# Splitting the next chunk's weights between the first chunk's tiles in a fused four-layer step

## Chip, cores and metric

The kernel runs on one core of a Trainium2 chip. The metric is the device time of one execution in microseconds. The time before is the median of three runs.

## What is computed

One inference step of a four-layer hybrid diffusion backbone on 128 context tokens and 512 latent tokens, model width 1024, all in fp32 accuracy. Layer 0 mixes tokens by pooling; layers 1 to 3 by attention (grouped-query, differential, windowed with a sink); each layer ends in a gated ConvFFN. The change touches the QKV projection of the three attention layers:

```python
qkv = h @ w_qkv                      # (640, 1024) @ (1024, 1536), and 3072 columns in layer 2
q, k = rmsnorm(q, qn), rmsnorm(k, kn)   # per head of 64
q, k = apply_rope(q, cos, sin), apply_rope(k, cos, sin)   # latent tokens only
```

## The kernel before

**Products.** Each fp32 product is made of three matmuls in a reduced format: `h_hi * w_hi`, `h_hi * w_lo` and `h_lo * w_hi`, where `hi` is the rounded value and `lo` what is left over. Weights come in chunks of 512 columns. A chunk is held as `UNITS` = 8 units of 128 partitions by 512 columns, one for each of the `KT` = 8 steps `k` of the contraction. ScalarE (ACT) writes `w_hi` of a unit as a rounded copy of `w_stage` (`split_w`, L2247), and VectorE (DVE) writes `w_lo` as `w_stage - w_hi` (`lo_w`, L2398). There is one buffer each for `w_stage`, `w_hi` and `w_lo`.

**QKV on TensorE (PE).** The 640 tokens are `NT` = 5 tiles of 128: tile 0 is the context, tiles 1 to 4 are latent. Layers 1 and 3 have 3 chunks (`QKV_CHUNKS`), layer 2 has 6. Tiles are counted on over the chunks: `i = c * NT + j`, and tile `i` goes to bank `i % 4` of `psA`. The first four tiles of the first chunk are computed side by side, step by step as `h` comes from the normalisation, and so end at once. From tile 4 on (token tile `j` = 4 of chunk 0) PE takes a tile at a time, 24 matmuls of 128x512 each (L2094, L2095, L2100). Tile `i` waits for the evacuation of tile `i - 4` (`s_qe`). At `j` = 0 each step `k` also waits for the `w_lo` of its unit (`s_wlo`). After step `k` of the last tile of a chunk PE raises `s_wused`, which says that unit `k` may be overwritten by the next chunk's.

**QKV on ACT.** For each tile in order: wait until it is computed, square it into `qkv_sq` (L2315, two buffers; the square of the normed tile `i` waits for the means of `i - 2`), and copy it from PSUM (L2316), which raises `s_qe`. Ahead of the last tile of a chunk come all eight `split_w` of the next chunk, each with a wait for its `s_wused`.

**QKV on DVE (`qkv_dve`, L1465).** For each normed tile: `means(i)` (L1494, L1497: the sum of squares of each head, scaled), and then `rotate(i - 1)`: multiply by the reciprocal root (L1506) and by the norm's weight (L1510, tile 0), or by cosines and sines and add (L1513, L1520 twice, L1523, latent tiles). Ahead of `means` of the last tile of a chunk come all eight `lo_w` of the next chunk. GpSimd (POOL) makes the reciprocal root between `means(i)` and `rotate(i)` with a power (L1945). `mark` (L1542) follows the last rotation and releases attention.

**Loads.** The sync engine's queue (SP) issues the load of the next half chunk into `w_stage` (L1806) once the `w_lo` of the four units that it overwrites are done.

Of the kernel before, what the change touches and what calls it, by code (L numbers as in the profile page):

```python
# [50 lines left out]
NT = (SEQ + DEC_SEQ) // P  # L51
# [5 lines left out]
UNITS = 8  # L57
# [69 lines left out]
def program(nc, t):  # L127
    with ExitStack() as ctx:
# [948 lines left out]
        def pool_pe(pe, product, mod_raw, mod_raw_sum):  # L1077
            pe.wait_ge(s_const, 1)
            pe.wait_ge(s_count, 16)
            for i, (c, _) in enumerate(EDGES):  # L1080
                ins = pe.matmul(psB[:, 2, i * 4 * EDGE:(i + 1) * 4 * EDGE].rearrange("p (g n) -> p g n", n=EDGE),
                                ones[0:1, :], inv_row[0:1, :, c:c + EDGE], start=True, stop=True)
# [382 lines left out]
        def qkv_dve(dve, own, lo_w, l):  # L1465

            nq = QKV_CHUNKS[l]
            kv = qkv[nq]
            c0 = FIRST_CHUNK[l]

            dve.wait_ge(s_rope, 16 * l)
            dve.wait_ge(s_small, 48)
            for i, r in ((0, R_QN), (1, R_KN)):
                g = row[:, r + (l - 1) * DH:r + l * DH]
                own(dve.tensor_tensor(rope_cos[:, i, :, :], rope_raw[:, 0, :, :],
                                      g.unsqueeze(1).to_broadcast([P, NT - 1, DH]), ALU.mult))

                for ax in range(2):
                    for hf in range(2):
                        a = ax * 32 + hf * 16  # L1480
                        b = ax * 32 + (1 - hf) * 16
                        own(dve.tensor_tensor(rope_sin[:, i, :, a:a + 16], rope_raw[:, 1, :, a:a + 16],
                                              g[:, b:b + 16].unsqueeze(1).to_broadcast([P, NT - 1, 16]), ALU.mult))
            if l == 3:

                dve.wait_ge(s_mask, 16)
                own(dve.tensor_copy(mask_r[:, :, :], mask_raw[:, :, :]))
                own(dve.tensor_copy(ident_r[:, :], ident[:, :]))
            own.wait()

            def means(i):
                c, j, n = NORMED[l][i]
                dve.wait_ge(s_qe[l], c * NT + j + 1)
                own(dve.tensor_reduce(qms[i % 2][:, 0:n],  # L1494
                                      qkv_sq[i % 2][:, 0:n * DH].rearrange("p (h n) -> p h n", n=DH), AX_X, ALU.add))
                own.wait()
                dve.tensor_scalar(qms[i % 2][:, 0:n], qms[i % 2][:, 0:n], 1.0 / DH, EPS, ALU.mult,  # L1497
                                  ALU.add).then_inc(s_qms[l], 1)

            def rotate(i):  # L1500
                c, j, n = NORMED[l][i]
                is_key = c >= 2
                x = kv[:, j, c * UNIT:c * UNIT + n * DH]
                xh = x.rearrange("p (h n) -> p h n", n=DH)
                dve.wait_ge(s_qrs[l], i + 1)
                own(dve.tensor_tensor(xh, xh, qrs[i % 2][:, 0:n].unsqueeze(2).to_broadcast([P, n, DH]), ALU.mult))  # L1506
                own.wait()
                if j == 0:
                    g = row[:, (R_KN if is_key else R_QN) + (l - 1) * DH:][:, 0:DH]
                    own(dve.tensor_tensor(xh, xh, g.unsqueeze(1).to_broadcast([P, n, DH]), ALU.mult))  # L1510
                    return
                ra, rb = rope_a[:, 0:n * DH], rope_b[:, 0:n * DH]
                own(dve.tensor_tensor(ra.rearrange("p (h n) -> p h n", n=DH), xh,  # L1513
                                      rope_cos[:, int(is_key), j - 1, :].unsqueeze(1).to_broadcast([P, n, DH]),
                                      ALU.mult))
                for hf in range(2):
                    def part(b, f):
                        return b.rearrange("p (h a f n) -> p h a f n", a=2, f=2, n=16)[:, :, :, f, :]
                    sn = rope_sin[:, int(is_key), j - 1, :].rearrange("p (a f n) -> p a f n", a=2, f=2)[:, :, hf, :]
                    own(dve.tensor_tensor(part(rb, hf), part(x, 1 - hf),  # L1520
                                          sn.unsqueeze(1).to_broadcast([P, n, 2, 16]), ALU.mult))
                own.wait()
                own(dve.tensor_tensor(x, ra, rb, ALU.add))  # L1523

            index = {(c, j): i for i, (c, j, _) in enumerate(NORMED[l])}
            done = 0
            for c in range(nq):
                for j in range(NT):
                    if j == NT - 1 and c < nq - 1:
                        for u in range(UNITS):  # L1530
                            lo_w(u, UNITS * (c0 + c + 1) + u + 1)
                    i = index.get((c, j))
                    if i is not None:
                        means(i)
                        if i:
                            rotate(i - 1)
                        done = i
            rotate(done)
            own.wait()

            dve.wait_ge(s_qe[l], nq * NT)
            dve.tensor_copy(mark[:, l:l + 1], ones2[:, 0:1]).then_inc(s_qkv, 1)  # L1542
# [701 lines left out]
        def _(act):  # L2244
            own = Steps(act, s_act)

            def split_w(c, units, waits=None):  # L2247

                for u in units:
                    if waits is not None:  # L2250
                        act.wait_ge(s_wused, waits + u + 1)
                    act.wait_ge(s_w[u // 4], c * 16 + 16)
                    act.activation(w_hi[:, u, :], w_stage[:, u, :], ACT.Copy).then_inc(s_whi, 1)  # L2253

            def square(n, d):

                l, second = n // 2, n % 2
                m = n - 1
                if n == 1:
                    act.wait_ge(s_mxxadd, d // 4 + 1)  # L2260
                if second:
                    act.wait_ge(s_mxadd[l], d + 1)
                    if d == 0 and l:
                        act.wait_ge(s_kv_out, 32 * l)
                else:
                    act.wait_ge(s_oadd[l - 1], KT * (ITERS - 1) + d + 1)
                if d >= 3:
                    act.wait_ge(s_sqsum, (KT - 2) * m + d - 2)
                dst = sq_sum if d == 0 else sq[d % 2]
                act.activation(dst[:, :], xT[:, d, :], ACT.Square).then_inc(s_sq, 1)  # L2270
# [20 lines left out]
            for l in range(DEPTH):  # L2291
                if l:
                    norm_act(2 * l)
                c0 = FIRST_CHUNK[l]
                if l == 0:
                    pool_act(act, own, split_w, square)
                else:
                    nq = QKV_CHUNKS[l]
                    kv = qkv[nq]
                    normed = {(c, j): (i, n) for i, (c, j, n) in enumerate(NORMED[l])}  # L2300
                    for c in range(nq):
                        for j in range(NT):
                            i = c * NT + j
                            if j == NT - 1 and c < nq - 1:
                                split_w(c0 + c + 1, range(UNITS), waits=UNITS * (c0 + c))
                            if j < NT - 1:
                                act.wait_ge(s_qp[l], c * (NT - 1) + j + 1)
                            else:
                                act.wait_ge(s_wused, UNITS * (c0 + c + 1))
                            ps = psA[:, i % 4, :]  # L2310
                            if (c, j) in normed:
                                k, n = normed[c, j]
                                if k >= 2:
                                    act.wait_ge(s_qms[l], k - 1)
                                own(act.activation(qkv_sq[k % 2][:, 0:n * DH], ps[:, 0:n * DH], ACT.Square))  # L2315
                            act.activation(kv[:, j, c * UNIT:(c + 1) * UNIT], ps, ACT.Copy).then_inc(s_qe[l], 1)  # L2316
                    act.wait_ge(s_qkv, l)
                    cw = c0 + nq
                    (attention_diff_act if l == 2 else attention_act)(act, own, l, lambda units: split_w(cw, units))
                    act.wait_ge(s_att[l], ATT_DONE[l])  # L2320
                    split_w(cw, range(4, UNITS))
                    for dt in range(KT):
                        split_w(cw + dt // 4 + 1, (2 * (dt % 4), 2 * (dt % 4) + 1), waits=UNITS * (cw + dt // 4))
                        if dt:
                            square(2 * l + 1, dt - 1)
# [480 lines left out]
```

## Time and profile before

| | us |
|---|---|
| median of three runs | 3190.6 (3188.68 to 3192.1) |
| profiled execution | 3182.12 |
| its span | 3180.3 |
| PE matmul busy | 3047.1 (96%) |
| DVE busy | 2079.8 (65%) |
| ACT busy | 1081.2 (34%) |
| POOL busy | 403.3 (13%) |
| mean granted TensorE clock | 0.980 |

The profiled execution is one run of the program, with its own time. The span is what the profile covers, from the first to the last instruction. Busy shares are averages over all stages; a wait in one stage doesn't show in them.

### The profile page before, as it was taken

How to read it: one execution, taken by the hardware profiler on the slowest of the kernel's cores; microseconds unless marked ns; L12 is line 12 of the kernel's file. 1: busy time of each engine (PE TensorE's matmuls, PEld its weight loads, DVE VectorE, ACT ScalarE, POOL GpSimd, SP SyncE). 2: the span in 40 equal slices, each digit the busy share in tenths (PEclk: the TensorE clock that was granted, in tenths of full speed). 3: DMA queues.
4: the chain of work that ended last, by engine and by line, in shares of the span. 5: the costliest groups of instructions: out<-in, count | busy, mean ns of one | idle time of the engine just before them, and what ended most of it. 6: DMA issues, size and time to landing. Idle time of an engine off the chain costs nothing.

```text
span 3180.3 us, 54564 instructions
## 1 busy us (share of the span) xinstructions
PE 3047.1 (96%) x21296; PEld 2779.6 (87%) x21296; DVE 2079.8 (65%) x4004; ACT 1081.2 (34%) x2250; POOL 403.3 (13%) x392
## 2 busy tenths in 40 slices
PE   8999999989999999998989899999999889999999
PEld 6899999866599999997865699999997668999999
DVE  7766666767756666667646576666667675766665
ACT  3322222326623222223335442222233563422221
POOL 3000000223310000003236410000012231000000
PEclk9999999989999999999988999999999899999999
DMA  8533323110033332321200223333221002222221
GB/s 339 210 119 123 128 92 127 53 57 1 2 119 133 119 124 101 119 106 45 80 31 6 82 86 116 117 132 119 101 106 53 4 1 83 77 80 67 73 71 47
DMA packets 47200, 290.15 MB, mean 91 GB/s; under 512 B 4946, under 2 KB 11346, under 8 KB 13266
## 3 DMA queue, kind: packets, MB, share of 16 engines
q1 hardware_dynamic: 47058, 288.21, 24.9%
q8 instruction: 95, 1.56, 0.2%
q14 instruction: 47, 0.38, 0.0%
HBM read 283.98 MB, written 4.21 MB: 91 GB/s over the span
## 4 chain that ended last, share of the span: by engine, by line
PE 88%; DVE 6%; ACT 2%; DMA 2%; issue 1%; POOL 0%; SPq 0%; POOLq 0%; DVEq 0%; ACTq 0%
PE psA L1980 38%; PE psB L1980 24%; PE psA L2094 3%; PE psA L2095 3%; PE psA L2100 3%; PE psB L1997 2%; PE psA L801 2%; PE psB L734 2%; PE psA L2171 1%; PE psB L716 1%; DMA w_stage<-weights_dram 1%; PE psA L702 1%; PE psB L859 1%; PE psA L2176 1%; DVE top L1589 1%
## 5 line engine op out<-in xcount | busy, mean ns | idle before, releaser
L1980 PE MATMUL psA<-h_hi,w_hi 128*128 128x320 f32 (+1 forms) x2736 | 624.9, 310 | 2.5 <-ACT u_raw L2336 1.7
L1980 PE MATMUL psA<-h_lo,w_hi 128*128 128x320 f32 (+1 forms) x2720 | 620.3, 309 | 0.0
L1980 PE MATMUL psA<-h_hi,w_lo 128*128 128x320 f32 x2704 | 616.2, 309 | 0.0
L2523 DVE SCALAR_TENSOR_TENSOR xT<-psB,mod,xT 128x128 f32<-128x128 f32 x750 | 377.7, 547 | 222.9 <-PE psB L1980 222.8
L1980 PEld LDWEIGHTS psA<-h_hi,w_hi 128*128 128x128 f32 x2736 | 456.2, 188 | 4.2 <-ACT u_raw L2336 2.5
L1980 PEld LDWEIGHTS psA<-h_lo,w_hi 128*128 128x128 f32 x2720 | 455.1, 188 | 0.0
L1980 PEld LDWEIGHTS psA<-h_hi,w_lo 128*128 128x128 f32 x2704 | 452.0, 188 | 0.0
L2582 DVE TENSOR_SCALAR conv<-u_raw,vec_sb 128x642 f32<-128x642 f32 x176 | 108.3, 615 | 438.9 <-ACT u_raw L2336 438.9
L2400 DVE TENSOR_TENSOR w_lo<-w_stage,w_hi 128x512 fp32r<-128x512 f32 x496 | 352.4, 755 | 36.3 <-ACT w_hi L2253 36.2
L1980 PE MATMUL psB<-g_hi,wo_hi 128*128 128x320 f32 x1280 | 299.3, 315 | 0.1
L1980 PE MATMUL psB<-g_hi,wo_lo 128*128 128x320 f32 x1280 | 295.2, 312 | 0.0
L1980 PE MATMUL psB<-g_lo,wo_hi 128*128 128x320 f32 x1280 | 292.0, 309 | 0.0
L2335 ACT ACTIVATE u_raw<-psA 128x128 f32<-128x128 f32 x176 | 49.2, 280 | 695.4 <-PE psA L1980 686.2
L1933 POOL TENSOR_TENSOR sq_sum<-sq_sum,sq 128x644 f32<-128x644 f32 x42 | 69.7, 1659 | 1662.3 <-ACT sq L2270 1660.2
L2365 ACT ACTIVATE wo_hi<-wo_stage 128x1024 fp32r<-128x1024 f32 x80 | 80.4, 1052 | 491.2 <-PE psB L1980 491.2
L1980 PEld LDWEIGHTS psB<-g_hi,wo_hi 128*128 128x128 f32 x1280 | 215.0, 189 | 12.6 <-issue 11.9
L1980 PEld LDWEIGHTS psB<-g_hi,wo_lo 128*128 128x128 f32 x1280 | 214.4, 188 | 0.0
L1980 PEld LDWEIGHTS psB<-g_lo,wo_hi 128*128 128x128 f32 x1280 | 214.0, 188 | 0.0
L2094 PE MATMUL psA<-w_hi,h_hi 128*128 128x512 f32 x480 | 191.0, 398 | 23.0 <-DVE w_lo L2400 18.4
L2341 ACT ACTIVATE w_hi<-w_stage 128x512 fp32r<-128x512 f32 x344 | 198.4, 633 | 0.0
L2095 PE MATMUL psA<-w_lo,h_hi 128*128 128x512 f32 x480 | 189.4, 395 | 0.0
L2100 PE MATMUL psA<-w_hi,h_lo 128*128 128x512 f32 x480 | 177.4, 394 | 0.0
(272 smaller groups left out, 4955.0 us busy)
## 6 DMA issues: line engine op xcount, KB each, us to landing
w_stage<-weights_dram SPq DMA_DIRECT2D x124, 1024.0 KB, 5.1
m_stage<-w_mod_dram SPq DMA_DIRECT2D x96, 1024.0 KB, 8.3
wo_stage<-w_out_dram SPq DMA_DIRECT2D x44, 1024.0 KB, 4.8
yT_dram<-xT SPq DMA_DIRECT2D x8, 322.0 KB, 2.2
xT<-xT_dram SPq DMA_DIRECT2D x1, 1544.0 KB, 10.5
xT<-xT_dram SPq DMA_DIRECT2D x1, 1032.0 KB, 7.0
w_stage<-weights_dram SPq DMA_DIRECT2D x2, 512.0 KB, 17.7
rope_raw<-rope_dram SPq DMA_DIRECT2D x3, 256.0 KB, 2.8
```

Of the source, the lines that this page charges most:

```text
L734: ins = pe.matmul(OUT_LAT[odd * DH:(odd + 1) * DH, x:y], value(kt, 2 * d // GROUP), pt[(2 * d + odd) % 4][:, kt - 1, x:y], start=(kt == CA ...
L801: ins = pe.matmul(psA[:, 2 * m + i, 0:n], x[r, q0:q0 + P], x[r, k0:k0 + n], start=True, stop=True)
L1933: pool.tensor_tensor(sq_sum[:, :], sq_sum[:, :], sq[d % 2][:, :], ALU.add).then_inc(s_sqsum, 1)
L1980: ins = pe.matmul(o, wp, xp[:, a:b], start=first and n == 0, stop=last and n == 2)
L2094: pe.matmul(o, hh, w_hi[:, k, :], start=(k == 0), stop=False)
L2095: pe.matmul(o, hh, w_lo[:, k, :], start=False, stop=False)
L2100: return pe.matmul(o, h_lo[:, k, col:col + P], w_hi[:, k, :], start=False, stop=(k == KT - 1))
L2341: act.activation(w_hi[:, u, :], w_stage[:, u, :], ACT.Copy).then_inc(s_whi, 1)
L2365: act.activation(wo_hi[:, f, :], wo_stage[:, f, :], ACT.Copy).then_inc(s_wohi, 1)
L2400: dve.tensor_tensor(w_lo[:, u, :], w_stage[:, u, :], w_hi[:, u, :].bitcast(F32), ALU.subtract).then_inc(s_wlo, 1)
L2523: ins = dve.scalar_tensor_tensor(out=xT[:, d, c:c + w], in0=tokens(ps, slot)[i], scalar=gate[:, d, i:i + 1], in1=xT[:, d, c:c + w], op0=AL ...
L2582: own(dve.tensor_scalar(o[:, 1:1 + n], u[:, 1:1 + n], vcol(v + 1), vcol(v + 3), ALU.mult, ALU.add))
```

## The change

On ACT the eight splits of the second chunk, which all stood ahead of the evacuation of tile 4, are spread: units 0 to 3 ahead of tile 2, units 4 and 5 ahead of tile 3, units 6 and 7 ahead of tile 4. On DVE the work of the first chunk is written out: `rotate(1)` and `rotate(2)` come behind all of the second chunk's `lo_w`, which are spread between `means` and `rotate(0)`. From `means(4)` on the order is what it was, as are the later borders between chunks. It holds in all three attention layers.

```diff
-            done = 0
+            done = 3
+
+            def next_lo(c, units):
+                for u in units:
+                    lo_w(u, UNITS * (c0 + c + 1) + u + 1)
+
+
+            means(0)
+            means(1)
+            next_lo(0, (0, 1))
+            rotate(0)
+            next_lo(0, (2, 3))
+            means(2)
+            next_lo(0, (4, 5, 6, 7))
+            rotate(1)
+            means(3)
+            rotate(2)
             for c in range(nq):
-                for j in range(NT):
-                    if j == NT - 1 and c < nq - 1:
-                        for u in range(UNITS):
-                            lo_w(u, UNITS * (c0 + c + 1) + u + 1)
+                for j in range(0 if c else NT - 1, NT):
+                    if c and j == NT - 1 and c < nq - 1:
+                        next_lo(c, range(UNITS))
                     i = index.get((c, j))
                     if i is not None:
                         means(i)
@@ ACT
                         for j in range(NT):
                             i = c * NT + j
-                            if j == NT - 1 and c < nq - 1:
-                                split_w(c0 + c + 1, range(UNITS), waits=UNITS * (c0 + c))
+
+                            between = {2: range(0, 4), 3: range(4, 6), 4: range(6, UNITS)} if c == 0 else {4: range(UNITS)}
+                            if c < nq - 1:
+                                split_w(c0 + c + 1, between.get(j, ()), waits=UNITS * (c0 + c))
```

## Rows read from the trace of the kernel before

**Rows 1.** The page: busy time by engine.
```profile
PE 3047.1 (96%) x21296; PEld 2779.6 (87%) x21296; DVE 2079.8 (65%) x4004; ACT 1081.2 (34%) x2250; POOL 403.3 (13%) x392
```
**Rows 2.** Line L2094, all layers: what ended PE's idle time (us, times).
```profile
  DVE w_lo L2400: 18.4, 3
```
**Rows 3.** Timeline, PE, layer 1: start us, us, instruction, [idle before <-releaser].
```profile
626.49 0.50 PE L2094 MATMUL psA<-w_hi,h_hi 128*128 128x512 f32 x1 [0.49 <-ACT qkv L2316]
...
631.84 0.39 PE L2100 MATMUL psA<-w_hi,h_lo 128*128 128x512 f32 x1
638.38 0.77 PE L2094 MATMUL psA<-w_hi,h_hi 128*128 128x512 f32 x1 [6.15 <-DVE w_lo L2400]
...
646.81 0.39 PE L2094 MATMUL psA<-w_hi,h_hi 128*128 128x512 f32 x1
...
652.25 0.39 PE L2094 MATMUL psA<-w_hi,h_hi 128*128 128x512 f32 x1
```
**Rows 4.** Timeline, PE, layer 2.
```profile
1474.60 0.39 PE L2100 MATMUL psA<-w_hi,h_lo 128*128 128x512 f32 x1
1481.13 0.77 PE L2094 MATMUL psA<-w_hi,h_hi 128*128 128x512 f32 x1 [6.15 <-DVE w_lo L2400]
...
1488.10 0.39 PE L2094 MATMUL psA<-w_hi,h_hi 128*128 128x512 f32 x1
```
**Rows 5.** Timeline, PE, layer 3.
```profile
2411.26 0.39 PE L2100 MATMUL psA<-w_hi,h_lo 128*128 128x512 f32 x1
2417.80 0.77 PE L2094 MATMUL psA<-w_hi,h_hi 128*128 128x512 f32 x1 [6.15 <-DVE w_lo L2400]
...
2425.70 0.39 PE L2094 MATMUL psA<-w_hi,h_hi 128*128 128x512 f32 x1
```
**Rows 6.** Stretches, layer 1: length, busy time by engine, PE clock, DMA share, GB/s.
```profile
632.20:638.38 6.18, 0.03 (x1) 0.03 (x1) 6.04 (x13) 2.51 (x5) 3.30 (x2) 0.67 0.00 0
638.38:644.49 6.11, 6.11 (x14) 4.78 (x15) 6.04 (x12) 0.00 (x0) 1.16 (x1) 0.50 0.55 189
```
**Rows 7.** Timeline, DVE, layer 1, first chunk border.
```profile
627.45 0.69 DVE L1494 TENSOR_REDUCE qms<-qkv_sq 128x8 f32<-128x512 f32 x1
...
629.18 0.69 DVE L1506 TENSOR_TENSOR qkv<-qkv,qrs 128x512 f32<-128x512 f32 x1 [0.83 <-POOL qrs L1945]
...
630.51 0.68 DVE L1494 TENSOR_REDUCE qms<-qkv_sq 128x8 f32<-128x512 f32 x1
...
631.31 0.69 DVE L1506 TENSOR_TENSOR qkv<-qkv,qrs 128x512 f32<-128x512 f32 x1
...
634.04 0.68 DVE L1494 TENSOR_REDUCE qms<-qkv_sq 128x8 f32<-128x512 f32 x1
...
637.55 4.90 DVE L2400 TENSOR_TENSOR w_lo<-w_stage,w_hi 128x512 fp32r<-128x512 f32 x8
```
**Rows 8.** Timeline, ACT, layer 1, first chunk border.
```profile
626.80 0.62 ACT L2316 ACTIVATE qkv<-psA 128x512 f32<-128x512 f32 x1
...
629.45 4.28 ACT L2253 ACTIVATE w_hi<-w_stage 128x512 fp32r<-128x512 f32 x8
633.62 0.61 ACT L2315 ACTIVATE qkv_sq<-psA 128x512 f32<-128x512 f32 x1
```
**Rows 9.** Timeline, POOL, layer 1: powers for tiles 0 and 1, and tile 2.
```profile
627.51 3.24 POOL L1945 TENSOR_TENSOR qrs<-qms,minus_half 128x8 f32<-128x8 f32 x2 [26.59 <-DVE qms L1497]
631.48 2.01 POOL L1945 TENSOR_TENSOR qrs<-qms,minus_half 128x8 f32<-128x8 f32 x1 [0.73 <-DVE qms L1497]
```
**Rows 10.** Timeline, DVE, layer 1, second chunk border.
```profile
664.45 0.69 DVE L1494 TENSOR_REDUCE qms<-qkv_sq 128x8 f32<-128x512 f32 x1 [1.83 <-ACT qkv L2316]
...
667.98 4.90 DVE L2400 TENSOR_TENSOR w_lo<-w_stage,w_hi 128x512 fp32r<-128x512 f32 x8
```
**Rows 11.** Timeline, PE, layer 1, second chunk border.
```profile
668.34 0.39 PE L2100 MATMUL psA<-w_hi,h_lo 128*128 128x512 f32 x1
668.81 0.47 PE L2094 MATMUL psA<-w_hi,h_hi 128*128 128x512 f32 x1
```
**Rows 12.** Timeline, SP, layer 1: loads of the third and fourth chunks.
```profile
640.07 33.16 SPq L1806 DMA_DIRECT2D w_stage<-weights_dram  x4
```

## The prediction

> **What bounds the kernel.** I read the page's busy times first. PE's matmuls take 96% of the span and no other engine more than 65% [rows 1], so the kernel gets faster only where PE stands still or runs slowly. The waits of the QKV line come next: over the whole run it waited three times for `w_lo`, 18.4 us in all [rows 2]. The timeline of PE shows one such wait in each attention layer, 6.15 us long, always between tile 4 (the last of the first chunk) and tile 5 (the first of the second) [rows 3 to 5].
>
> The wait has a tail. In the stretch in which PE stood still the granted clock falls to 0.67 in the mean, and in the 6.11 us behind it it is 0.50, PE's lower level of 1.2 GHz [rows 6]. That stretch holds 14 matmuls, 0.44 us each instead of the 0.227 worked out below.
>
> The timeline of DVE says why `w_lo` is late. ACT has written all eight `w_hi` by 629.45 + 4.28 = 633.7 [rows 8], but DVE is in its queue order: `means(2)`, `rotate(1)`, `means(3)`, `rotate(2)` from 630.51 to 637.55, and only then the eight `w_lo` [rows 7]. PE goes on 0.15 us after the first of them ends (637.55 + 0.68 = 638.23, against 638.38). The wait is DVE's order and nothing else.
>
> **What the wait costs.** At full clock a tile lasts from 646.81 to 652.25, 5.44 us for 24 matmuls, so 0.227 each [rows 3]. In layer 1 the last matmul of tile 4 starts at 631.84, tile 5 was due at 632.07 and its successor at 637.51. That successor starts at 646.81: 9.30 us lost, 6.31 in the wait and 2.99 in the slow clock [rows 3]. Layer 2 in the same way: due 1474.60 + 0.23 + 5.44 = 1480.27, came at 1488.10, 7.83 us (6.30 and 1.53) [rows 4]. Layer 3: due 2416.93, came at 2425.70, 8.77 us (6.31 and 2.46) [rows 5]. Together 25.9 us, of which 7.0 are clock. The Trainium skill ("TensorE: Matmul & The Clock Gate", section "Wait — 56ns, not 53.3ns?") gives 215.7 ns between such matmuls at the upper level and 426.7 at the lower; the trace shows 227 on the upper and about 440 over the slow stretch. With the page's figures a tile would be due 0.27 us sooner and each layer would have lost that much more; the row is used.
>
> **The change, part by part, in layer 1.** No instruction is added or removed: the same eight `split_w`, eight `lo_w`, `means` and `rotate` are issued in another order. Steps between starts, from rows 7 and 8: a split 0.52 us (629.45 to 633.62 for eight), an evacuation (square and copy) about 0.97, a `lo_w` 0.61 (4.90 for eight), `means` 0.80 (630.51 to 631.31), `rotate(0)` 1.33 (629.18 to 630.51), a latent `rotate` 2.73 (631.31 to 634.04).
>
> ACT: the second tile's copy ends at 627.42 [rows 8]. Unit `k` is free when step `k` of tile 4 is through, that is from about 627.5 on, one every 0.68 us [rows 3]. So the splits of units 0 to 3 follow PE and end at 628.1, 628.8, 629.5 and 630.2; tile 2 is evacuated by 631.2, units 4 and 5 are split by 631.7 and 632.2, tile 3 is evacuated by 633.2, units 6 and 7 are split by 633.7 and 634.2, tile 4 is evacuated by 635.2.
>
> DVE: `means(1)` from 627.45 to 628.3 [rows 7]; `lo_w` 0 ends at 628.9 and 1 at 629.5, both paced by ACT. `rotate(0)` needs the first power, which before let it start at 629.18 [rows 7, 9], and so doesn't wait: it ends at 630.8. `lo_w` 2 and 3 end at 631.5 and 632.1, `means(2)` at 632.9 (its tile is in by 631.2), and `lo_w` 4 to 7 at 633.5, 634.1, 634.7 and 635.3.
>
> PE needs unit `k` at 632.07 + 0.68 `k`: 632.1, 632.8, 633.4, 634.1, 634.8, 635.5, 636.2, 636.8. With 0.15 us of signalling the slack is 3.0, 3.1, 1.8, 1.9, 1.1, 1.2, 1.3 and 1.4 us. The whole wait goes, and with it what made the clock fall. The least slack, 1.1 us at unit 4, is the cover of this step: beyond it each us that DVE is late costs a us in each layer.
>
> Moved past: the evacuations of tiles 2 and 3 come up to 3.7 us later (633.2 against about 629.5). They release the banks of tiles 6 and 7, which PE wants at 637.5 and 643.0: hidden, with over 6 us to spare. Tile 5's square waits for `means(3)`, now at 638.8, so its copy is done near 640.0; its bank is wanted at 653.8 by tile 9. SP's loads of the third chunk are released by `lo_w` 3 and 7 and so come some 8 us sooner than 640.07 [rows 12], over idle DMA engines (share 0.00 [rows 6]), and nothing waits for them. These are costed at nothing.
>
> What is late next is DVE. Behind `lo_w` 7 at 635.3 it has `rotate(1)`, `means(3)`, `rotate(2)`, `means(4)`, `rotate(3)`, 9.8 us, to 645.1, while PE is already in tile 7. Each tile costs DVE 3.5 us (2.1 where the rotation is the context's) against PE's 5.44, so it catches up: `means(5)` and `rotate(4)` to 648.6, `means(6)` and `rotate(5)` to 650.7, `means(7)` and `rotate(6)` to 654.2. `means(8)` can start 1.3 us after PE begins tile 9 (before: 664.45, with tile 9 begun at 652.25 + 2 x 5.44 = 663.13 [rows 3, 10]), now at 653.8 + 1.3 = 655.1. DVE is there 0.9 us ahead. From there on the second border repeats itself, with its small wait of 0.24 us (668.81 instead of 668.34 + 0.23 [rows 11]), which is neither gained nor lost.
>
> One unknown is contention. In the new order `lo_w` 0 and 1 (two SBUF inputs) run beside POOL's second power. Nearest row: `rotate(0)`'s multiply at 629.18, also with two SBUF inputs, ran beside that power and took 0.69 us, no more than alone [rows 7, 9]. So the cost is taken as nothing; the other end is that `lo_w` 0 waits for both powers to end, at 627.51 + 3.24 = 630.75. The Trainium skill speaks against the change here ("SBUF — State Buffer", section "Who interferes with whom"): a DVE instruction with two SBUF inputs contends with a GpSimd instruction that reads SBUF, and the later one blocks fully. The row at 629.18 shows no block. By the rule `lo_w` 0 would start at 630.75 and the time would be rival B's.
>
> **Sum.** 9.30 + 7.83 + 8.77 = 25.9 us. The profiled execution would go from 3182.1 to 3156.2 us. The median of the runs shown is 8.5 us above it; the waits are fixed by instruction order, so the same difference is taken off: 3190.6 - 25.9 = 3164.7 us, 0.81% less.
>
> **Rivals.** A measurement of this kernel can tell about 0.2% (6.4 us) from no change.
>
> A, the forecast: all three waits and their slow tails go. 3164.7 us, between 3162 and 3168, since the slow tail was 1.5 to 3.0 us by layer and slow stretches elsewhere may shift by as much. Chance 0.80.
>
> B, a shorter wait stays: `lo_w` is held back by POOL's powers or by hand-overs between ACT and DVE. `lo_w` 0 at 630.75 instead of 628.3 puts all of DVE 2.4 us back; the least slack of 1.1 leaves 1.3 us of PE wait in each layer, 3.9 us in all: 3168.6 us, and up to 3175 if part of the clock's fall comes back. For it: the hand-overs are many. Against: the row at 629.18. Chance 0.12.
>
> C, the wait moves to the second border: the rotations put off are not caught up. Above 0.9 us of lateness at `means(8)`, each us is a us of PE wait. If DVE is there 2 us later than worked out, 1.1 us is left over in each layer, 3.3 us in all: 3168; if it also brings the clock down, 3175. Against: DVE had 1.83 us of idle time ahead of a tile in this stretch before [rows 10]. Chance 0.04.
>
> D, nothing is gained: PE would find another wait of the same length, as for the later evacuations of tiles 2 and 3, which would need to be over 6 us later than worked out. 3190 us, chance 0.02.
>
> E, slower: the same queue of DVE as in C, but so far behind that the second border costs more than the first gave. That starts where a layer loses 8.6 us of gain and 2.1 more, so DVE would be over 7 us late at `means(8)` (a slow clock of up to 3 us making up the rest). It is 0.9 us early by the sum. 3200 us, chance 0.02.
>
> The range is 3159 to 3174 us. A and most of B and C lie in it. Faster 0.95, same 0.03, slower 0.02.
>
> **What the profile after should show.** No wait for `w_lo` of 6 us on the QKV line in any layer, at most the small ones of later borders. Granted clock of 1.00 from tile 4 to tile 6. First `w_lo` of the second chunk ahead of `rotate(0)`, and the last of them some 1.4 us before PE's last step needs it. DVE without idle time until tile 8 is evacuated, then the old rhythm. PE's QKV stage in layers 1, 2 and 3 shorter by about 9.3, 7.8 and 8.8 us, the stages behind it unchanged in length. The prediction is wrong if a wait of over 1 us stands at a step of tile 5, or at tile 10, or if the attention stage grows by what QKV lost.

## The result, and the profile after

The change makes the kernel faster: median 3160.66 us (3158.31 to 3163.56, four runs) against 3189.64 us (3186.57 to 3192.1, four runs), 29.0 us less. The ratio is 0.991, 95% interval 0.9893 to 0.9927. The profiled execution took 3158.31 us against 3182.12, 23.8 less. The forecast was 3164.7 us, 25.9 less.

The QKV line of PE (L2094 before, L2109 now) has no wait for `w_lo` in any layer; before it had three, of 18.4 us together [rows 2]. What ended the idle time there, in us and times (this view counts matmuls and weight loads together):

```profile
L2109 PE MATMUL psA<-w_hi,h_hi x480: 387/389/496, 607.0 to 2450.0; 128*128 128x512 f32 x160
its engine sat idle before it (us, times) until:
...
  ACT qkv L2333: 2.8, 4
  ACT h_hi L2296: 2.7, 3
```

The timeline of PE in layer 1 answers to [rows 3]: the first matmul of tile 4, the last one of it and the first two of tile 5, and the first of tile 6.

```profile
629.54 0.50 PE L2109 MATMUL psA<-w_hi,h_hi 128*128 128x512 f32 x1 [0.50 <-ACT qkv L2333]
...
634.90 0.39 PE L2115 MATMUL psA<-w_hi,h_lo 128*128 128x512 f32 x1
635.12 0.39 PE L2109 MATMUL psA<-w_hi,h_hi 128*128 128x512 f32 x1
635.35 0.39 PE L2110 MATMUL psA<-w_lo,h_hi 128*128 128x512 f32 x1
...
640.57 0.39 PE L2109 MATMUL psA<-w_hi,h_hi 128*128 128x512 f32 x1
```

Tile 5 starts 0.22 us behind the last matmul of tile 4, where 6.5 us stood before. From the first matmul of tile 4 to that of tile 6 it is 11.03 us; before it was 646.81 - 626.49 = 20.32 [rows 3]. The granted clock in tile 5 and behind it, with the columns of [rows 6]:

```profile
634.90:641.08 6.18, 6.18 (x29) 5.12 (x28) 6.08 (x13) 3.33 (x7) 2.01 (x1) 1.00 0.78 239
641.08:646.00 4.92, 4.92 (x23) 4.07 (x22) 4.75 (x11) 1.09 (x2) 2.56 (x2) 1.00 0.30 127
```

The timeline of DVE in layer 1, against [rows 7], and of ACT, against [rows 8]:

```profile
630.50 0.69 DVE L1494 TENSOR_REDUCE qms<-qkv_sq 128x8 f32<-128x512 f32 x1
...
631.30 1.29 DVE L2417 TENSOR_TENSOR w_lo<-w_stage,w_hi 128x512 fp32r<-128x512 f32 x2
632.50 0.69 DVE L1506 TENSOR_TENSOR qkv<-qkv,qrs 128x512 f32<-128x512 f32 x1
...
633.84 1.28 DVE L2417 TENSOR_TENSOR w_lo<-w_stage,w_hi 128x512 fp32r<-128x512 f32 x2
635.04 0.68 DVE L1494 TENSOR_REDUCE qms<-qkv_sq 128x8 f32<-128x512 f32 x1
...
635.83 2.50 DVE L2417 TENSOR_TENSOR w_lo<-w_stage,w_hi 128x512 fp32r<-128x512 f32 x4
...
658.20 0.69 DVE L1494 TENSOR_REDUCE qms<-qkv_sq 128x8 f32<-128x512 f32 x1 [0.86 <-ACT qkv L2333]
```

```profile
630.53 2.71 ACT L2268 ACTIVATE w_hi<-w_stage 128x512 fp32r<-128x512 f32 x4
...
634.10 1.15 ACT L2268 ACTIVATE w_hi<-w_stage 128x512 fp32r<-128x512 f32 x2
...
636.09 1.16 ACT L2268 ACTIVATE w_hi<-w_stage 128x512 fp32r<-128x512 f32 x2
...
641.95 0.60 ACT L2332 ACTIVATE qkv_sq<-psA 128x512 f32<-128x512 f32 x1 [3.71 <-DVE qms L1497]
```

Layer 1 runs 3.05 us later in this execution (tile 4 at 629.54 instead of 626.49). With that taken off, the last `lo_w` ends at 638.33 - 3.05 = 635.28; the prediction had 635.3. The last row of DVE shows it idle for 0.86 us ahead of tile 8's `means`; the prediction had 0.9. The last row of ACT is tile 5's square, which now waits for `means(3)` and holds up nobody.

The gain is inside the QKV stage. Read off the two profiled executions, in us, from the first QKV matmul to `mark`:

| | before | full change |
|---|---|---|
| layer 1 | 97.23 | 87.93 |
| layer 2 | 173.91 | 166.07 |
| layer 3 | 96.69 | 87.95 |
| sum | 367.83 | 341.95 |

That is 25.9 us less. What lies outside of these stages took 3180.3 - 367.8 = 2812.5 us before and 2814.6 after, 2.1 us more. The change doesn't touch it. 3.05 us of difference lies ahead of the first QKV matmul, which starts at 603.97 before and at 607.02 now; in the first 200 us the granted clock was 0.98 before and 0.96 in this execution. In two further executions of the changed kernel (e0b_full_change and e0_full_change below) it was 0.98 and 0.97 there, and that matmul starts at 603.66 and 605.46.

### The profile page after: what moved, and what is told of

The parts are those of the page before. It is cut to its first block, busy times and chain, and to the rows that moved or that the text cites. A ratio compares the mean times of both kernels' runs of the same rounds, so it can differ in the third digit from the quotient of the medians.

```text
span 3156.5 us, 54564 instructions
## 1 busy us (share of the span) xinstructions
PE 3043.1 (96%) x21296; PEld 2777.9 (88%) x21296; DVE 2078.7 (66%) x4004; ACT 1081.3 (34%) x2250; POOL 403.6 (13%) x392
## 4 chain that ended last, share of the span: by engine, by line
PE 89%; DVE 5%; ACT 2%; DMA 1%; issue 1%; SPq 0%; POOL 0%; DVEq 0%; ACTq 0%
PE psA L1995 38%; PE psB L1995 24%; PE psA L2109 4%; PE psA L2110 3%; PE psA L2115 3%; PE psB L2012 2%; PE psA L801 2%; PE psB L734 2%; PE psA L2186 1%; DMA w_stage<-weights_dram 1%; PE psB L716 1%; PE psB L859 1%; PE psA L702 1%; PE psA L2191 1%; DVE w_lo L2417 1%
## 5 line engine op out<-in xcount | busy, mean ns | idle before, releaser
L2109 PE MATMUL psA<-w_hi,h_hi 128*128 128x512 f32 x480 | 187.8, 391 | 4.6 <-ACT h_hi L2296 2.7
## 6 DMA issues: line engine op xcount, KB each, us to landing
w_stage<-weights_dram SPq DMA_DIRECT2D x2, 512.0 KB, 18.3
```

Source lines behind the costliest of these rows:

```text
L2109: pe.matmul(o, hh, w_hi[:, k, :], start=(k == 0), stop=False)
```

## Experiments

Each kernel was run beside the kernel before on the same chip, five rounds each. "Full change" is the changed kernel. The kernel before had a median of 3184.16 us on the chip of the first group, 3186.03 on that of the second, 3187.57 on that of the third.

**The full change, twice more** (e0_full_change in the second group, e0b_full_change in the third).

> The full change as it is, for the same chip and the same runs of the kernel before as the others. Theory 1 (25.9 us of waits and slow clock at the first chunk border are gone, nothing is given back elsewhere): 25.9 us below the kernel before, give or take 3 us of what varies outside of this stretch. Theory 2 (part of the gain is given back in the attention stages): under 22 us.

> The full change again, as the measure for the two others on this chip: 25.9 us below the kernel before, as the first time.

Measured: 3160.18 us, 25.9 below the kernel before (ratio 0.9921, interval 0.9909 to 0.9933), and 3158.85 us, 28.7 below (0.9911, 0.9898 to 0.9925). Nothing is given back. That the difference of medians lies between 25.9 and 29.0 while the stages give 25.9 in each trace shows how far medians scatter here. The slower executions of one kernel are mostly those with the lower mean clock: of the 17 of the kernel before in the first group the fastest took 3178.38 us at 0.983 and the slowest 3190.87 us at 0.976. One place is layer 2's attention (see e4b_filled_wait below).

**DVE's order alone** (e1_dve_only), in the full change:

```diff
-                            between = {2: range(0, 4), 3: range(4, 6), 4: range(6, UNITS)} if c == 0 else {4: range(UNITS)}
-                            if c < nq - 1:
-                                split_w(c0 + c + 1, between.get(j, ()), waits=UNITS * (c0 + c))
+                            if j == NT - 1 and c < nq - 1:
+                                split_w(c0 + c + 1, range(UNITS), waits=UNITS * (c0 + c))
```

> DVE's new order alone; ACT again splits all eight units of the second chunk ahead of tile 4. Theory 1 (the wait was DVE's order, the rotations ahead of w_lo): ACT's eight splits start after tile 3's evacuation, so lo_w 0 and 1 are paced by them and DVE ends some 1.8 us later than with the full change; by the slack of 1.1 us at unit 4 a wait of about 0.7 to 0.8 us stays in each layer, so about 23.5 us below the kernel before. Theory 2 (both halves are needed, w_lo only comes early if the splits do): less than half of the gain, 13 us or less.

Measured: 3165.88 us, 18.3 below the kernel before (ratio 0.9943, 0.993 to 0.9956). The QKV stages take 88.87, 167.00 and 88.84 us, 23.1 less than before, against the 23.5 expected. The median gained 5 us less than expected; that rest lies outside of the stages. From the first matmul of tile 4 to that of tile 6 it takes 11.78, 11.82 and 11.82 us, 0.75 to 0.8 above the full change, and from tile 6 to tile 10 another 0.15 to 0.2 us. DVE's timeline in layer 1 shows that it waits for ACT:

```profile
630.16 1.29 DVE L2416 TENSOR_TENSOR w_lo<-w_stage,w_hi 128x512 fp32r<-128x512 f32 x2 [1.79 <-ACT w_hi L2268]
```

The order on DVE is nearly all of the change; the splits between the tiles are worth some 2.8 us. The median asks for more than the stages show, 5.7 us above the second group's full change, but that is on another chip.

**ACT's order alone** (e2_act_only), in the kernel before:

```diff
-                            if j == NT - 1 and c < nq - 1:
-                                split_w(c0 + c + 1, range(UNITS), waits=UNITS * (c0 + c))
+                            between = {2: range(0, 4), 3: range(4, 6), 4: range(6, UNITS)} if c == 0 else {4: range(UNITS)}
+                            if c < nq - 1:
+                                split_w(c0 + c + 1, between.get(j, ()), waits=UNITS * (c0 + c))
```

> ACT's new order alone; DVE keeps rotate(1), means(3), rotate(2) ahead of all lo_w. Theory 1: nothing gained; means(2) waits for the later evacuation of tile 2 and all behind it comes about 0.7 us later, so PE's wait for w_lo grows from 6.15 to about 6.9 us and the kernel is about 2 us slower than before. Theory 2: about half of the gain, 13 us faster than before.

Measured: 3188.65 us, ratio 1.001 (1.0001 to 1.0018): slower by 0.3 to 5.7 us, as expected by theory 1. The QKV stages are 2.6 us longer in all than before. The wait is 6.83 us in each layer instead of 6.15; here is layer 1:

```profile
640.61 0.77 PE L2094 MATMUL psA<-w_hi,h_hi 128*128 128x512 f32 x1 [6.83 <-DVE w_lo L2401]
```

Theory 2 falls with these two runs: the halves are not equal, and the ACT half by itself does harm.

**The slack of the middle units** (e3_rotate1_first), in the full change:

```diff
-            next_lo(0, (4, 5, 6, 7))
             rotate(1)
+            next_lo(0, (4, 5, 6, 7))
```

> The full change, but rotate(1) (2.73 us) stands ahead of lo_w 4 to 7. If the slack at unit 4 is the 1.1 us of the prediction, a wait of 1.6 us appears in each layer at the fourth step of tile 5, in the middle of a running stretch, too short for the clock to fall: 4.9 us above the full change, 21 to 24 us below the kernel before. The rival (the slack was larger, other waits set tile 5) gives no difference to the full change; the rival that any wait at this place brings the slow clock back gives 10 us or more above the full change.

Measured: 3164.63 us, ratio 0.9943 (0.9929 to 0.9956), 19.5 below the kernel before. One wait per layer, in the middle of tile 5, for `w_lo`:

```profile
637.18 0.50 PE L2109 MATMUL psA<-w_hi,h_hi 128*128 128x512 f32 x1 [1.29 <-DVE w_lo L2417]
637.51 0.39 PE L2110 MATMUL psA<-w_lo,h_hi 128*128 128x512 f32 x1
637.75 0.39 PE L2115 MATMUL psA<-w_hi,h_lo 128*128 128x512 f32 x1
637.97 0.39 PE L2109 MATMUL psA<-w_hi,h_hi 128*128 128x512 f32 x1
```

Tile 4 to tile 6 takes 12.60, 12.63 and 12.62 us, 1.6 above the full change, as expected, and the stages are 4.8 us longer than there (4.9 expected). The median, 19.5 us below the kernel before, is outside of the 21 to 24 expected of it; the difference lies outside of the stages. So the slack at unit 4 was 2.73 - 1.6 = 1.1 us, and the matmuls behind so short a wait start 0.23 us apart: no slow clock. Both rivals fall.

**Filler in the wait, too long** (e4_filled_wait), in the kernel before:

```diff
                             pe.wait_ge(s_qe[l], i - 3)
+                            if i == NT:
+                                keep_on(52, psA[:, 1, :])
```

> The kernel before, with 52 small matmuls of 128 columns (0.113 us each, 5.9 us) whose results are overwritten, issued by PE ahead of the wait for w_lo at tile 5. They cover the idle time and do nothing for its length. If the tail behind the wait is the clock's, as the prediction has it, the wait of 6.2 us stays in length, the matmuls behind it start 0.227 us apart from the first, and the kernel is 7.0 us (1.5 to 3.0 by layer) faster than before. If the slow matmuls behind the wait have another cause, such as w_lo coming only as fast as DVE makes it, it makes no difference.

Measured: 3199.77 us, 15.6 slower (ratio 1.0052, 1.004 to 1.0064). The expectation was wrong by a factor of two: each fp32 call of the filler shows as two matmuls in the timeline, so that it ran 5.5 us past the wait:

```profile
632.11 11.77 PE L2038 MATMUL psA<-ones,ident_sb 128*128 128x128 f32 x104
643.63 0.48 PE L2094 MATMUL psA<-w_hi,h_hi 128*128 128x512 f32 x1
643.95 0.40 PE L2095 MATMUL psA<-w_lo,h_hi 128*128 128x512 f32 x1
```

It settles nothing about what the slow clock costs. The matmuls behind it run at full clock. In the traced execution the QKV stages are 8.9 us longer than before; what more the median shows lies outside of them and is not explained.

**Filler of the right length** (e4b_filled_wait): as above with 26 calls.

> The kernel before with 26 calls of the filler ahead of the wait for w_lo at tile 5; the trace of the run with 52 calls shows two matmuls for each, 0.113 us apiece, so this is 5.9 us of matmuls inside the 6.2 us wait. Theory 1 (the tail behind the wait is the clock's): from the first matmul of tile 4 to the first of tile 6 it takes 17.3 us in every layer (10.9 and the wait of 6.3), against 20.3, 18.9 and 19.8 before, and the kernel is 7 us faster than before. Theory 2 (the tail has another cause, such as w_lo coming only as fast as DVE makes it): no difference.

Measured: 3178.16 us, 7.9 below the kernel before (ratio 0.9979, 0.997 to 0.9988). Tile 4 to tile 6 takes 17.41, 17.41 and 17.42 us, where before it was 20.32, 18.85 and 19.79, so 6.7 us less in the three; the stages are 6.8 us shorter in all. The wait is as long as before, only filled:

```profile
632.21 5.96 PE L2038 MATMUL psA<-ones,ident_sb 128*128 128x128 f32 x52
638.41 0.50 PE L2094 MATMUL psA<-w_hi,h_hi 128*128 128x512 f32 x1 [0.24 <-DVE w_lo L2402]
638.75 0.40 PE L2095 MATMUL psA<-w_lo,h_hi 128*128 128x512 f32 x1
638.99 0.39 PE L2100 MATMUL psA<-w_hi,h_lo 128*128 128x512 f32 x1
```

The first matmul of tile 5 starts at 638.41, as at 638.38 in [rows 3], and those behind it 0.23 to 0.24 us apart. So `w_lo` came fast enough all along, and the tail of 7 us was the clock's. The traced execution was the slowest of the eleven, 3183.88 us. It shows where such an execution loses its time: from `mark` of layer 2 to layer 3's first QKV matmul it takes 769.1 us, in the kernel before 762.8, and nothing is changed there. The clock was granted differently. The 180 us behind that `mark`, of this kernel and then of the one before (0.81 and 0.86 are the clock):

```profile
1616.90:1796.90 180.00, 160.40 (x713) 102.58 (x713) 117.90 (x329) 88.36 (x208) 115.81 (x127) 0.81 0.04 12
```

```profile
1620.60:1800.60 180.00, 160.35 (x738) 101.61 (x739) 119.38 (x334) 92.11 (x214) 118.10 (x129) 0.86 0.04 12
```

**A larger backlog on DVE** (e5_backlog), in the full change:

```diff
             rotate(2)
+            own.wait()
+            for _ in range(5):
+                own(dve.tensor_tensor(rope_a[:, 0:UNIT], rope_b[:, 0:UNIT], rope_b[:, 0:UNIT], ALU.mult))
+                own.wait()
```

> The full change with five more multiplications of 128x512 on DVE behind rotate(2), 3.6 us of work whose result isn't used. DVE had 0.9 us in hand at tile 8's means in the trace of the full change. If the prediction's account of the backlog is right, PE waits 2.7 us at tile 10 in each layer: 8.2 us above the full change, and up to 15 if such a wait brings the slow clock back. If DVE's backlog is no limit at this border, no difference to the full change.

Measured: 3173.98 us, 13.8 above the full change on the same chip (ratio to the kernel before 0.9958, 0.9944 to 0.9971). The wait is at tile 10 in all three layers, 2.87, 2.86 and 2.88 us; here are layers 1 and 3:

```profile
663.19 0.47 PE L2113 MATMUL psA<-w_hi,h_hi 128*128 128x512 f32 x1 [2.87 <-DVE w_lo L2421]
...
2432.43 0.47 PE L2113 MATMUL psA<-w_hi,h_hi 128*128 128x512 f32 x1 [2.88 <-DVE w_lo L2421]
...
2434.44 0.63 PE L2114 MATMUL psA<-w_lo,h_hi 128*128 128x512 f32 x1
2434.87 0.63 PE L2119 MATMUL psA<-w_hi,h_lo 128*128 128x512 f32 x1
```

Tile 6 to tile 10 takes 24.8 us in all layers instead of 22.0: 2.8 each, 2.7 expected. In layer 3 alone the matmuls behind it drop to 0.43 us apart for a while, which costs another 1.6 us; the same wait in layers 1 and 2 left the clock alone. The stages are 10.0 us longer in all (90.70, 168.83, 92.35), the rest of the 13.8 is outside of them and not explained. The second border is a limit, and DVE had 3.6 - 2.8 = 0.8 us in hand there, about the 0.9 of the prediction.

**The next wait of the same kind** (e6_filled_mark, e6b_filled_mark): in the full change, PE stands still for 5.1 us in layers 1 and 3 until `mark`.

```diff
+                    if l != 2:
+                        keep_on(22, psB[:, 3, :])
                     if l == 2:
                         attention_diff_pe(pe, l, proj_first)
```

> The full change, with 22 calls of the filler (44 matmuls, 5.0 us) in PE's wait of 5.1 us for the mark at the end of the QKV stage in layers 1 and 3. If the slow stretch at the head of attention (granted clock 0.53 and 0.72 in two of its stretches of 6 us in layer 1) comes from that wait, it goes, and the kernel is 2 to 4 us faster than the full change. If the later waits of attention's start bring the clock down by themselves, or ACT and DVE set the pace there, no difference.

> The filler in the wait for the mark again. The first time it was 4.0 us below the full change in the median, but mark to next layer took 743.9 us in its trace against 743.5. If the gain was real: 3 to 5 us below the full change again. If it was scatter: within 2 us of it.

Measured: 3156.17 us, 4.0 below the full change of its group (ratio to the kernel before 0.9902, 0.9888 to 0.9915), and 3153.25 us, 5.6 below that of its group (0.9893, 0.9878 to 0.9908). The 5.6 us are a little more than the 3 to 5 expected. The first time the ranges of the two kernels overlap (3150.04 to 3159.47 against 3155.03 to 3165.62), the second time they don't (up to 3154.92 against 3155.55 and more). From the first transposition of a key in layer 1 to the first scores it takes 699.37 - 693.48 = 5.9 us instead of 699.63 - 691.85 = 7.8 in the full change, whose lines come first (e0b_full_change, then e6b_filled_mark):

```profile
691.85 1.06 PE L630 MATMUL psB<-ident_sb,qkv 128*64 128x128 f32 x4 [5.11 <-DVE mark L1557]
...
699.63 0.63 PE L676 MATMUL psA<-key_hi,query 128*128 128x320 f32 x1 [2.74 <-DVE query L1560]
```

```profile
693.48 0.63 PE L630 MATMUL psB<-ident_sb,qkv 128*64 128x128 f32 x4 [0.20 <-DVE mark L1557]
...
699.37 0.41 PE L676 MATMUL psA<-key_hi,query 128*128 128x320 f32 x1 [2.74 <-DVE query L1560]
```

The traces don't place the rest of the gain. From `mark` to the next layer's first QKV matmul (in layer 3: to the end), layers 1 and 3 together take 1446.8 and 1442.4 us with the filler, against 1444.4 and 1444.3 in the full change of the same groups. What the traced executions gained lies mostly behind `mark` in layer 2, 761.3 and 761.9 us against 765.3 and 767.1, and there no filler was put in. The granted clock in the 180 us behind that `mark` was 0.89 and 0.87 with the filler, 0.86 and 0.84 without; the first execution of the full change, also without, had 0.86 and took 762.4 us. So the medians say that the kernel got faster, twice; that the filler at the mark alone did it, and how, is not shown.

**Both waits at attention's start filled** (e7_filled_both): the same, and in `attention_pe`:

```diff
             query_prep(0)
+            for _ in range(12):
+                pe.matmul(psA[:, 0, 0:P], ident[:, :], ones[:, :], start=True, stop=True)
```

> The filler in the wait for the mark and 24 more small matmuls (2.7 us) in the wait for the first query in layers 1 and 3. If slow clock at the head of attention costs time, this is 1 to 3 us faster than the filler at the mark alone. If ACT and DVE set the pace there, no difference, whatever the clock.

Measured: 3149.68 us (3148.25 to 3153.03), ratio to the kernel before 0.9883 (0.9868 to 0.9898). That is 9.2 us below the full change of its group and 37.9 below the kernel before, the fastest of all versions; against the filler at the mark alone it is 3.6 us, somewhat more than the 1 to 3 expected, with ranges that just touch. Here the traces do place it: layers 1 and 3 behind `mark` take 1437.4 us together, 6.9 less than in the full change of this group and 5.0 less than with the filler at the mark alone (1.4 in layer 1 and 3.6 in layer 3). It isn't in the second wait itself: in layer 1 the first scores come 5.9 us behind the first transposition with or without the second filler. The stretches of 6, 9 and 7 us from 6 us ahead of `mark` on in layer 1, of the full change and then of this kernel (length, PE busy, clock, DMA share, GB/s):

```profile
685.64:691.64 6.00, 1.10 (x5) 0.80 0.00 0
691.64:700.64 9.00, 6.05 (x26) 0.69 0.09 30
700.64:707.64 7.00, 5.46 (x33) 0.84 0.00 0
```

```profile
687.38:693.38 6.00, 6.00 (x49) 1.00 0.00 0
693.38:702.38 9.00, 7.52 (x58) 1.00 0.09 30
702.38:709.38 7.00, 6.18 (x36) 0.76 0.00 0
```

The clock is whole over `mark` and falls a little later, in a stretch in which attention has waits of 1.22 and 0.82 us for ACT.

## Why the prediction was right

**The cause of the wait.** Right. The two halves apart show it: DVE's order takes 23.1 of 25.9 us out of the stages, ACT's makes the wait longer (6.83 us).

**What the wait cost.** 25.9 us by the sum, 25.9 us in the stages, layer by layer 9.30, 7.84 and 8.74 against the 9.30, 7.83 and 8.77 of the text. The 7.0 us of clock in it measured 6.8 in the stages and 7.9 in the median when the wait alone was filled. One reading was loose: 0.44 us for each slow matmul is a mean that takes in the first gap of 0.57 us. Behind it they start 0.427 us apart. The sum doesn't use it.

**The order of the border.** Right to within 0.1 us for the last `lo_w`, the slack at unit 4 (1.1 us) and DVE's reserve at tile 8 (0.86 against 0.9 us). Each of the last two was also measured by using it up.

**Contention, rival B.** DVE wasn't held back: the `lo_w` pair at 631.30 took 1.29 us, no more than two of them take elsewhere (0.61 and 0.68), and `rotate(0)` began right behind it at 632.50. But the prediction looked only at DVE, and it was POOL that gave way. Its two powers took 3.52 us in the full change and 3.24 both before and with DVE's order alone, where the second power began while DVE stood still:

```profile
630.56 3.52 POOL L1960 TENSOR_TENSOR qrs<-qms,minus_half 128x8 f32<-128x8 f32 x2 [26.59 <-DVE qms L1497]
```

```profile
627.53 3.24 POOL L1960 TENSOR_TENSOR qrs<-qms,minus_half 128x8 f32<-128x8 f32 x2 [26.57 <-DVE qms L1497]
```

Apart they are 1.64 and 1.92 us in the full change, the same in all three layers. The second starts at 632.16 while `lo_w` 1, begun at 631.90, is still running. Most powers of the QKV stages start 0.17 us into a multiplication of DVE's, and take 2.01 us. A power that starts while DVE is idle or in a reduction takes 1.64. The Trainium skill ("SBUF — State Buffer", section "Who interferes with whom") says that a DVE instruction with two SBUF inputs contends with a GpSimd instruction that reads SBUF, and that the order of issue decides which of them is held up. The traces agree where DVE was first: the power takes longer by about what was left of DVE's instruction. They don't where the power was first: both `lo_w` began while the first power ran, and were not held up. The powers read only 8 elements per partition, so a large one may act otherwise, and no run here tried that. Nothing waited for the 0.28 us, so the sum stands; that contention costs DVE nothing here was the right number with half of the picture.

**Rival C** was a real limit 0.9 us away, and rival E its far end. D didn't occur.

**The size.** The median came out 4.0 us below the forecast and the profiled execution 2.1 us above it. The median is inside the stated range, but 1.3 us below the 3162 to 3168 that rival A had for itself. No step of the sum accounts for either. The interval of the ratio, 0.9893 to 0.9927, is 23.3 to 34.1 us, so the measured 29.0 can't be told from 25.9. The time outside the QKV stages differed from one profiled execution to the next by as much: 2812.5 us before, 2814.6 in the full change, 3163.2 - 344.7 = 2818.5 with DVE's order alone. The stages test the sum, to within 0.1 us; how near the median came is in part luck: the forecast took the profiled execution's distance from the median, 8.5 us, as fixed, and in the full change it measured 3160.66 - 3158.31 = 2.4 us.

## What to carry to other kernels

Where one engine prepares the next operand and also does work that nobody waits for yet, its queue order is the wait: put the work with the near deadline first, and work out when the backlog has to be gone. Order the producer's producer as well, but see that it is not the only thing that is moved. A long wait of PE can cost its length and a slow clock behind it as well; where the wait can't be shortened, matmuls whose results are overwritten, sized from the timeline to end just before it does, give the second part back.

## What was not expected of the hardware

One fp32 call of the filler shows in the trace as two matmuls, 0.115 us each (5.96 us for the 52 of 26 calls). Waits of 6.15 us brought the clock down in all three layers; waits of 1.29 us in none, and waits of 2.87 us in one of three, so that the same wait cost 2.8 or 4.4 us. A small POOL instruction that starts while DVE is in an instruction with two SBUF inputs took up to 0.5 us longer (2.11 against 1.64), and DVE's took 0.69 as ever. With both waits at attention's start filled in layers 1 and 3, the kernel took 9.2 us less in the median, and in the traced executions 6.9 us of the difference stood behind `mark` in these layers.
